# The first input projection of a two-layer diffusion trunk: conditioning by quarters of the columns, between pairs of k tiles

## What is computed

```python
ms = jnp.split(jax.nn.silu(c) @ ada_w[l] + ada_b[l], 6, axis=-1)       # conditioning, latent tokens
mc = jnp.split(jax.nn.silu(c_ctx) @ ada_w[l] + ada_b[l], 6, axis=-1)   # the same for context tokens
h_lat = modulate(rmsnorm(x_lat, pre_mix_g[l]), ms[0], ms[1])           # h * (1 + scale) + shift
h_ctx = modulate(rmsnorm(x_ctx, pre_mix_g[l]), mc[0], mc[1])
p_lat = h_lat @ w_in[l]                                                # 1024 -> 2560
```

## Time and profile before

| what | value |
|---|---|
| median of 3 runs | 1900.32 us |
| the profiled execution | 1897.9 us |
| its span, first to last instruction | 1896.1 us |
| TensorE matmul busy | 1737.1 us (92%) |
| VectorE busy | 1419.9 us (75%) |
| ScalarE busy | 1099.0 us (58%) |
| mean granted TensorE clock | 0.96 of full speed |
| loaded and stored by DMA | 505.78 MB |

### The profile page before, as it was taken

One profiled execution on the slowest core, in us unless ns is written; L12 is line 12 of the kernel. 1 busy time (PEld: TensorE's weight loads), 2 busy tenths in 40 slices (PEclk: granted clock), 3 DMA queues, 4 the chain that ended last, 5 costly groups with the idle time before them and its releaser, 6 DMA issues.

```text
span 1896.1 us, 24119 instructions
## 1 busy us (share of the span) xinstructions
PE 1737.1 (92%) x7944; PEld 1401.0 (74%) x7944; DVE 1419.9 (75%) x1663; ACT 1099.0 (58%) x1408; POOL 41.2 (2%) x73
## 2 busy tenths in 40 slices
PE   5988898999999969766899999999999999999993
PEld 2865676887878858555688888888888888888883
DVE  3746756655754585664699999999999999999994
ACT  3344345222222253444688888888888888888883
POOL 1000000000010000101000000000000000000000
PEclk8998998999999989977899999999999999999997
DMA  9825343656664516334799999999999999999992
GB/s 321 235 64 167 133 135 108 225 159 209 220 207 148 166 54 196 115 114 152 265 389 361 390 384 365 394 357 391 383 363 393 361 386 381 370 393 358 387 379 89
DMA packets 225423, 505.78 MB, mean 267 GB/s; under 512 B 16376, under 2 KB 39056, under 8 KB 225088
## 3 DMA queue, kind: packets, MB, share of 16 engines
q1 hardware_dynamic: 221120, 493.30, 72.8%
q0 software_dynamic: 4224, 11.47, 2.3%
HBM read 497.34 MB, written 19.96 MB: 273 GB/s over the span
## 4 chain that ended last, share of the span: by engine, by line
issue 53%; PE 34%; DVE 7%; ACT 3%; DMA 2%; SPq 0%; POOL 0%; POOLq 0%; ACTq 0%; DVEq 0%
PE ps L552 10%; PE ps L554 10%; PE ps L553 10%; DVE w_lo L1292 1%; DMA raw<-in_ffn_w 1%; PE ps L742 1%; PE ps L614 1%; PE ps L577 1%; DMA raw<-in_ada_w 1%; DVE xs L1463 1%; DVE acc L1308 1%; ACT w_hi L990 1%; DVE att L1543 1%; DVE pr L1537 0%; PE ps L712 0%
## 5 line engine op out<-in xcount | busy, mean ns | idle before, releaser
L1292 DVE TENSOR_TENSOR w_lo<-raw,w_hi 128x1024 fp32r<-128x1024 f32 x570 | 685.0, 1222 | 226.1 <-ACT w_hi L990 192.2
L1204 ACT ACTIVATE w_hi<-raw 128x1024 fp32r<-128x1024 f32 x448 | 473.9, 1062 | 105.7 <-PE ps L554 105.7
L552 PE MATMUL ps<-w_hi,he_hi 128*128 128x512 f32 x896 | 354.4, 396 | 0.7 <-DVE he_lo L1692 0.7
L554 PE MATMUL ps<-w_hi,he_lo 128*128 128x512 f32 x896 | 350.0, 391 | 0.0
L553 PE MATMUL ps<-w_lo,he_hi 128*128 128x512 f32 x896 | 349.4, 390 | 0.0
L1292 DVE TENSOR_TENSOR w_lo<-raw_more,w_hi 128x1024 fp32r<-128x1024 f32 x224 | 273.9, 1225 | 45.9 <-ACT w_hi L1204 26.8
L1204 ACT ACTIVATE w_hi<-raw_more 128x1024 fp32r<-128x1024 f32 x224 | 237.7, 1062 | 53.5 <-PE ps L554 53.5
L990 ACT ACTIVATE w_hi<-raw 128x1024 fp32r<-128x1024 f32 x122 | 128.7, 1063 | 225.4 <-PE ps L554 217.7
L554 PEld LDWEIGHTS ps<-w_hi,he_lo 128*128 128x128 f32 x896 | 168.6, 188 | 36.0
L552 PEld LDWEIGHTS ps<-w_hi,he_hi 128*128 128x128 f32 x896 | 168.6, 188 | 34.8 <-issue 1.0
L553 PEld LDWEIGHTS ps<-w_lo,he_hi 128*128 128x128 f32 x896 | 168.8, 188 | 33.9
(11 more groups left out here) (216 smaller groups left out, 1983.7 us busy)
## 6 DMA issues: line engine op xcount, KB each, us to landing
raw<-in_moe_w SPq DMA_DIRECT2D x448, 512.0 KB, 6.0
raw_more<-in_moe_w SPq DMA_DIRECT2D x224, 512.0 KB, 6.0
raw<-in_ada_w SPq DMA_DIRECT2D x96, 512.0 KB, 4.4
raw<-in_ffn_w SPq DMA_DIRECT2D x66, 512.0 KB, 5.0
raw<-in_w_in SPq DMA_DIRECT2D x40, 512.0 KB, 4.9
raw<-in_w_out SPq DMA_DIRECT2D x16, 512.0 KB, 4.4
yrows<-in_x SPq DMA_DIRECT2D x8, 512.0 KB, 8.1
xe<-xrows SPq DMA_DIRECT2D x8, 512.0 KB, 6.3
```

Source lines behind the costliest of these rows:

```text
L552: pe.matmul(o, lh, rh, start=start, stop=False)
L554: return pe.matmul(o, ll, rh, start=False, stop=stop)
L1204: act.activation(w_hi[:, s % SPL, :], expert_raw(i), ACT.Copy).then_inc(hi_done, 1)
L1292: dve.tensor_tensor(w_lo[:, s_ % SPL, :], src, w_hi[:, s_ % SPL, :].bitcast(F32), ALU.subtract)\
```

## The change

The conditioning of layer 0's first norm is cut into four pieces by quarters of the columns: piece q holds shift and scale of columns 256q to 256q+255, which is what k tiles 2q and 2q+1 need. Its four units are 4 k tiles x 256 columns each (rows of 1 KB where they were 2 KB); a unit has four matmuls of 256 columns. The unit order becomes: piece 0, weight unit 0, piece 1, weight unit 1, and so on. x and ctx are issued ahead of unit 0. TensorE goes through the first projection in `project_first`, two k tiles at a time, with the units of the next piece spread over the 24 matmuls, and the transposes of the next two k tiles after the first k tile. The transposes write banks 4 and 5 in turn. `ada_finish` has three instructions for a piece. ScalarE has a Sqrt on one element after the Silus, so that the table load comes there. VectorE does the norm first, and then for each piece the copy, the finish, the low part of the weight unit (`take`) and the split of two k tiles.

```diff
-ADA_SEQ = [(0, p, h) for p in (0, 1, 3, 4) for h in range(2)]
+ADA_SEQ = [(0, 0, q) for q in range(4)] + [(0, p, h) for p in (3, 4) for h in range(2)]
...
+    def ada_quarter(q):
+        for part in range(2):
+            for h in range(2):
+                add(("ada", q), tall(ada_w[0], 4 * h, 4, D * part + 256 * q, 256), False, (4, 256))
...
+                if l + jn == 0:
+                    ada_quarter(u)
                 project(j, u, u + 1)
...
-                if u.k == 4:
+                if u.k == 0:
                     for b in range(NB):
                         sp.dma_start(xs[:, b, :], ...).then_inc(s_x, 16)
...
+                    if c < 4:
+                        n = 256 * (u.a % 4 // 2)
+                        for q in range(4):
+                            m = pe.matmul(ps[32 * q:32 * q + 32, bank, n:n + 256], cstat[:, 4 * (u.a % 2) + q, :], w[:, q, :],
+                                          start=(u.a % 2 == 0), stop=(u.a % 2 == 1), tile_position=(0, 32 * q))
+                        m.then_inc(ada_used, 1)
+                        continue
...
+            def project_first():
+
+                ada_rows(0, ADA)
+                ada_turn(0, ADA)
+                turn_h("mix0", NB, (0, 1))
+                for q, u in enumerate(at["in", 0, IN_ORDER[0]]):
+                    pe.wait_ge(lo_done, u.s + 1)
+                    h, lo = (view(t, u) for t in split_at(u.s))
+                    for kk in range(2):
+                        k = 2 * q + kk
+                        pe.wait_ge(sg("hT mix0"), k + 1)
+                        for b in range(NB):
+                            m = mm3(ps[:, b, :], hT_hi[:, k, P * b:P * b + P], hT_lo[:, k, P * b:P * b + P],
+                                    h[:, kk, :], lo[:, kk, :], k == 0, k == KD - 1)
+                            if k % 2 and b == NB - 1:
+                                m.then_inc(unit_used, 1)
+                            if q < 3 and b % 2:
+                                ada_rows(q + 1, ADA, [2 * kk + b // 2])
+                        if q < 3 and kk == 0:
+                            pe.wait_ge(sg("hT32 mix0"), 2 * q + 2)
+                            turn_h("mix0", NB, (2 * q + 2, 2 * q + 3))
+                    if q < 3:
+                        ada_turn(q + 1, ADA)
...
+            act.activation(st2[:, 127:128], cst[:, C_ONES:C_ONES + 1], ACT.Sqrt)
...
                     if key == "mix0":
-                        act.wait_ge(sg("ada fin"), 3 + k // 4)
+                        if k % 2 == 0:
+                            split_upto(first_units[key] + k // 2)
+                            act.wait_ge(sg("ada fin"), k // 2 + 1)
...
+                if c < 4:
+                    def pair(i):
+                        return pcol[:, 0, i + 2 * c:i + 2 * c + 2].unsqueeze(2).to_broadcast([P, 2, 2])
+                    b, a = mod_b[:, 0, 0, 2 * c:2 * c + 2, :], mod_a[:, 0, 0, 2 * c:2 * c + 2, :]
+                    dve.tensor_tensor(b, new[:, 0:2, :], pair(0), ALU.add)
+                    link(dve.tensor_tensor(a, new[:, 2:4, :], pair(KD), ALU.add))
+                    dve.scalar_tensor_tensor(out=a, in0=a, scalar=1.0, in1=pair(48), op0=ALU.add, op1=ALU.mult).then_inc(sg("ada fin"), 1)
+                    return
...
+            prenorm("mix0", NB, lambda b: None)
             for c in range(4):
-                if c == 2:
-                    prenorm("mix0", NB, lambda b: None)
-                if c == 3:
-                    split_h("mix0", range(4))
                 ada_copy(c, ADA)
                 ada_finish(c, ADA)
-            split_h("mix0", range(4, KD))
+                take(at["in", 0, IN_ORDER[0]][c].k + 1)
+                split_h("mix0", (2 * c, 2 * c + 1))
```

More of the change, by code:

```diff
@@ L146, in ada @@
                 add(("ada", n), tall(ada_w[l], 2 * u, 2, D * part + 512 * half, 512), False, (2, 512))
-    ada(0, 4)
+    def ada_quarter(q):
+        for part in range(2):
+            for h in range(2):
+                add(("ada", q), tall(ada_w[0], 4 * h, 4, D * part + 256 * q, 256), False, (4, 256))
     for l in range(2):
@@ L371, in program, with hT_bank @@
         ADA = 6
+        def hT_bank(key, k):
+            return 4 + k % 2 if key == "mix0" else k
         acc_end = [sum(KD * streams(i) for i in range(n + 1)) for n in range(len(PARTS))]
@@ L613, in turn_h @@
                     for k in ks:
-                        m = pe.transpose(ps[:, k, P * b:P * b + P], xn[:, b, P * k:P * k + P], ident)
+                        m = pe.transpose(ps[:, hT_bank(key, k), P * b:P * b + P], xn[:, b, P * k:P * k + P], ident)
                         if b == nb - 1:
                             m.then_inc(sg("hT ps " + key), 1)
+            def project_first():
[20 more added lines that the diff above has]
+                        ada_turn(q + 1, ADA)
             def project_in(l):
-                pe.wait_ge(sg("ada fin"), 4)
                 ctx, lat = len(qk[l]) - 2 * NLAT, len(qk[l])
+                if l == 0:
+                    project_first()
                 for jn, j in enumerate(IN_ORDER[:3]):
+                    if l + jn == 0:
+                        continue
                     if jn >= 2:
@@ L946, in _ @@
             pe.wait_ge(sg("pcol"), 2)
-            for c in range(4):
-                if c == 3:
[L949 to L953, removed]
             for l in range(2):
@@ L1034, in modulate_h @@
                     for r in range(nb // 2):
-                        ins = act.activation(hT32[:, k, 256 * r:256 * r + 256], ps[:, k, 256 * r:256 * r + 256], ACT.Identity,
+                        ins = act.activation(hT32[:, k, 256 * r:256 * r + 256], ps[:, hT_bank(key, k), 256 * r:256 * r + 256], ACT.Identity,
                                              bias=mod_b[:, l, which, k, r:r + 1], scale=mod_a[:, l, which, k, r:r + 1])
                     ins.then_inc(sg("hT32 " + key), 1)
[L1038 to L1044, removed]
+                    if key in first_units and key != "mix0" and k % 2:
+                        split_upto(first_units[key] + k // 2)
             def post_squares(key, half, srcs, junk_, ready):
@@ L1437, in split_h @@
                         .then_inc(sg("hT " + key), 1)
-                    if k % 2 and (k > 4 or key != "mix0"):
-                        split_upto(first_units[key] + (k // 2 - 2 if key == "mix0" else k // 2))
+                    if k % 2 and key != "mix0":
+                        split_upto(first_units[key] + k // 2)
             def post_gates(key, half, which, dst, srcs):
```

## The result

The changed kernel took 1910.99 us (median of 6 runs, 1907.4 to 1912.09) against 1900.42 for the kernel before (median of 6, 1899.07 to 1906.37): ratio 1.0056, 95% interval 1.0044 to 1.0068. It is slower by 0.56%, 10.6 us. The profiled executions took 1907.4 and 1897.9 us, 9.5 apart. The forecast was 1908.2 in a range from 1903 to 1914.

The account below looks back on a forecast made before the run. TensorE was taken to bound the kernel: 25.2 + 3 x (9.45 + 5.0) + 5.5 = 74.05, plus 1.46 and 3.7 for the clock, gave 79.2 against 71.33, +7.9 us. Forecast 1908.2 us, range 1903 to 1914.

Parts of the forecast that it names:

- T: When ScalarE begins to copy out the first projection's sums: 71.33 us in the kernel before, forecast 79.2.
- The first start: Start of the first projection, after loading, turn and transposes: forecast at 25.2 us, against 47.88 before.
- Rounds and gaps without the clock: First projection: three rounds of two k tiles at 9.45 us, each followed by a 5.0 us wait for the chain.
- The last round without the clock: The first projection's last 24 matmuls, with no conditioning or transposes between them: 5.5 us.
- The clock: TensorE at half clock at all four round starts: 1.46 us lost at the first, 3.7 over the other three.
- "One for one": Behind the first projection: a shift of T carries undiminished to the kernel's end, since units, order and work are the same.
- The forecast's first reading: Profile page: the chain that ended last is TensorE's, its issue and matmuls together 87%.
- (1): Gaps between rounds: the clock holds through them; T +4.2 or +3.0 us, 1903.3 to 1904.5 us; chance 0.18.
- (2): Rounds: switching matmul widths makes conditioning dear, 6.9 us more; +14.8 us, 1915 us; chance 0.11.
- (3): Rounds: conditioning matmuls run for nothing beside the projection's and the clock stays full; -4.8 us, 1895.5 us; chance 0.04.
- (4): Loading: a piece or weight unit arrives late in a round, about 4.4 us per late tile; +12 us; chance 0.05.

Follow-up runs that it names:

- e2: The changed kernel with the next piece's four conditioning tiles among the first k tile's matmuls and the turn before the second's; ratio 0.9965 to the kernel before.
- e1: The changed kernel with extra matmuls that compute nothing filling TensorE's three gaps between rounds; 1903.18 us, ratio 1.0019 to the kernel before.
- e8: The kernel of e2 with extra matmuls that compute nothing in the opening, before the first projection; 1886.69 us, ratio 0.9928 to the kernel before.
- e5: The changed kernel with the next piece's four conditioning tiles in one block after a round's 24 projection matmuls; 1907.80 us, ratio 1.0037 to the kernel before.
- e9: The kernel of e8 with the next piece's four conditioning tiles in one block after the first k tile's 12 matmuls; 1884.59 us, ratio 0.9925 to the kernel before.
- e7: The changed kernel, unchanged, traced a second time; first projection's sums copied from 85.40 us, span 1907.3 us.
- e4: The kernel before with only x and ctx issued ahead of conditioning unit 0 instead of unit 4; 1899.49 us, ratio 1.0000 to the kernel before.

## Why the prediction was right, and where a term was not

The forecast was slower by 7.9 us; it is 10.6 by the medians, inside the range. Its mechanism is shown: the projection starts 21.5 us earlier and loses it again, and 12.8 more, in three gaps that hold the whole chain from conditioning sum to split (14 us; e2 takes the gaps away by another order of the same instructions, and gains 17 us with the clock that they cost), in conditioning and transposes that now stand between the projection's matmuls (about 11), and in the clock (about 9 more than before; e1).

Step by step for T, forecast 79.2 and measured 84.14:

- **The first start**, 25.2: measured 26.38, +1.2. The tiles came when forecast (copy at 19.65, measured 19.72); the turn was priced by a row at full clock and the transposes by one in which the clock fell midway, and both ran at half. e8 gives 24.63 with the clock high.
- **Rounds and gaps without the clock**, 43.35: three rounds of 12.02, 12.14 and 12.21 and three gaps of 4.78 are 50.7, less half of the 5.52, 5.90 and 6.06 us at half clock, 8.7, gives 42.0: -1.4. The gap is 4.78 and not 5.0, since the weight unit's low part is hidden behind ScalarE and the added finish instruction is cheaper; the round at full clock is 9.44 in e1, where 9.45 was forecast. That the round came out so well is two errors that cancel: a piece costs not 2.5 but about 2.9 us (by e5 and e9, 1.9 for the block and 0.3 for each of three more switches), and the transposes 1.09 rather than 1.45.
- **The last round without the clock**, 5.5: 7.06 less 1.41 is 5.65, +0.15.
- **The clock**, 1.46 + 3.7 = 5.2: half of 5.52, 5.90, 6.06 and 2.82 is 10.15, **+5.0. This is the term that was mis-sized.** Half is a little too much: a projection matmul follows the last after 0.43 us at half clock and 0.23 at full, and by e1's round and the gaps (3 x 9.44 + 3 x 4.78 = 42.7) the rounds and gaps are off by -0.7 and the clock by +4.3. I had taken a mean of 2.45 us from three rises, the shortest of which (0.45 us) came after transposes had already run for 3.2 us, so it was no price for a start out of a gap, and had put my upper bound at 4.0 (2.0 lost). Here the four took 2.8 to 6.1, three of them above that bound; in e7's trace all four did (5.3 to 6.1). That the clock would fall in every gap was right. The Trainium skill ("TensorE: Matmul & The Clock Gate", HAM oscillation) describes a kernel that waits after every k tile and so starts every one at half rate. This trace agrees, four starts of four, though it waits after two k tiles, and for other engines rather than for DMA.

The sum at T was 5 us too small. "One for one" behind T was wrong by -3.5 us in the two pairs of traces: there the clock makes stages 1 to 2 us longer or shorter with the same work. Two errors of opposite sign brought the forecast of the time (+7.9) nearer to the result (+10.6) than T alone would have: that part is luck. The forecast's first reading was also stronger than its row: the page gives 53% of the chain as "issue" without naming an engine; the finish line rests on the earlier trace rows, and they held.

The rivals: the clock did not hold through the gaps (1). Conditioning inside the projection was not dear at the 6.9 us priced (2): the switches do cost, but three in a round 1 us, 3 us in all. Faster because conditioning runs for nothing (3) fell: a round costs what its parts cost. A late tile (4) is in no round of the trace: nothing in the rounds waits for DMA. The missing idea was that this order can be mended without giving up the interleaving: with the piece one k tile earlier, the change that lost 0.56% wins 0.35%.

## What to carry to other kernels

When work is interleaved so that it can start earlier, look at what comes out of its last instruction: if the next round needs it through a chain over several engines, the producer has to stand half a round ahead, or each round pays the whole chain. Price a gap on TensorE with two terms, its length and the half clock behind it; here three gaps cost 14 us in themselves (3 of them turns, which have to be done anyway) and some 7 in clock. Filling gaps with matmuls that compute nothing is a cheap test for the second term, and ahead of the first projection they were worth keeping (e8 against e2).

## What was unexpected of the hardware

- After a gap of 4.78 us the clock took 5.90 and 6.06 us to come back in rounds with conditioning tiles between the matmuls, and 2.82 in the last one without. But what stands in the round doesn't decide it: in the second trace of the same kernel the last round took 6.10, and in e5, whose rounds begin with 12 unbroken matmuls, the four starts took 3.5, 5.6, 3.5 and 5.7. The time is not fixed, and no run here shows what sets it.
- The turn's 8 instructions took 1.05 us at full clock and 1.86 at half, the 8 transposes 1.09 and 1.95: small TensorE steps in a chain also pay for the clock.
- A change of TensorE from 128-column to 32-column matmuls and back costs about 0.3 us (0.95 us for three in e5, 1.02 for three at full clock in e9).
- Tiles with rows of 1 KB came at 352 GB/s where those with 2 KB came at 386 and 387 (20 to 26 us in the changed kernel, the kernel before and e4).
- The view of the clock shows 1.00 before the first change that the trace holds, also where matmuls ran at half clock (26.38 to 31.90 in the changed kernel).
